# A mixture of experts in one order by load: dense, 128-slot and 64-slot members in place of nine equal ones

## What is computed

```python
def moe_swiglu(h, router, w_gate, w_up, w_down):
    logits = (hf @ router).astype(jnp.float32)
    top_v, top_i = lax.top_k(logits, TOP_K)          # 2 of 8
    top_w = jax.nn.softmax(top_v, axis=-1)
    # gates: for each token the two weights, at its two experts
    for e in range(N_EXPERTS):
        y = y + gates[:, e:e + 1] * swiglu(hf, w_gate[e], w_up[e], w_down[e])
```

## Time and profile before

| | us |
|---|---|
| median of 3 runs | 1819.85 (1819.36 to 1824.78) |
| profiled execution | 1821.17 |
| its span | 1819.4 |
| first expert product on PE | 901.57 |
| last down product on PE | 1797.11 |

### The profile page before, as it was taken

The page is one execution under the profiler, slowest core; times in us unless marked ns, Lnnn a source line. Parts: engine busy times, 40 slices in busy tenths (PEclk is TensorE's granted clock), DMA queues, the critical chain, the costliest instruction groups (busy, mean ns, idle before and its releaser), DMA issues.

```text
span 1819.4 us, 20970 instructions
## 1 busy us (share of the span) xinstructions
PE 1689.4 (93%) x8417; PEld 1387.7 (76%) x8418; DVE 1388.9 (76%) x1442; ACT 910.9 (50%) x837; POOL 0.2 (0%) x4
## 2 busy tenths in 40 slices
PE   4988999999999797797799999999999999999995
PEld 1876777788888596466688888888888888888884
DVE  5858657776777845674488988889798989888896
ACT  5431232211122334332477777777677777777773
POOL 0000000000000000000000000000000000000000
PEclk9988999999999898899699999999999999999998
DMA  9533334444567132100299999999999999999992
GB/s 352 195 136 126 113 127 149 139 163 161 170 223 242 53 117 70 47 1 24 68 337 342 358 346 343 358 337 360 344 341 350 354 335 357 341 348 356 334 366 88
DMA packets 214552, 426.32 MB, mean 234 GB/s; under 512 B 8186, under 2 KB 64028, under 8 KB 214452
## 3 DMA queue, kind: packets, MB, share of 16 engines
q1 hardware_dynamic: 210218, 420.37, 65.9%
q10 hardware_dynamic: 4234, 4.57, 0.8%
HBM read 423.86 MB, written 1.05 MB: 234 GB/s over the span
## 4 chain that ended last, share of the span: by engine, by line
PE 88%; DVE 6%; ACT 2%; issue 1%; DMA 1%; SPq 1%; DVEq 0%; ACTq 0%
PE bank L504 26%; PE bank L506 25%; PE bank L505 25%; PE bank L1740 2%; PE bank L1795 2%; PE bank L1729 2%; DVE lo L463 2%; PE bank L1834 1%; PE bank L1515 1%; DMA raw<-in_ada_w_dram 1%; PE bank L1746 1%; PE bank L1509 1%; ACT hi L457 1%; PE bank L1868 0%; PE bank L1869 0%
## 5 line engine op out<-in xcount | busy, mean ns | idle before, releaser
L463 DVE TENSOR_TENSOR lo<-raw,hi 128x2048 fp32r<-128x2048 f32 x361 | 820.8, 2282 | 199.4 <-ACT hi L457 198.0
L457 ACT ACTIVATE hi<-raw 128x2048 fp32r<-128x2048 f32 x361 | 689.7, 1912 | 474.9 <-PE bank L506 454.3
L504 PE MATMUL bank<-hi,xgh 128*128 128x512 f32 (+1 forms) x864 | 328.8, 381 | 5.0 <-DVE lo L463 5.0
L506 PE MATMUL bank<-hi,xgl 128*128 128x512 f32 (+1 forms) x864 | 325.3, 377 | 0.0
L505 PE MATMUL bank<-lo,xgh 128*128 128x512 f32 (+1 forms) x864 | 325.3, 377 | 0.0
L504 PEld LDWEIGHTS bank<-hi,xgh 128*128 128x128 f32 x864 | 163.0, 189 | 36.6 <-issue 5.2
L506 PEld LDWEIGHTS bank<-hi,xgl 128*128 128x128 f32 x864 | 163.1, 189 | 33.0
L505 PEld LDWEIGHTS bank<-lo,xgh 128*128 128x128 f32 x864 | 163.1, 189 | 31.3
L504 PE MATMUL bank<-hi,aTh 128*128 128x512 f32 x396 | 159.0, 402 | 0.0
L506 PE MATMUL bank<-hi,aTl 128*128 128x512 f32 x396 | 154.7, 391 | 0.0
L505 PE MATMUL bank<-lo,aTh 128*128 128x512 f32 x396 | 154.4, 390 | 0.0
(11 more groups left out here) (315 smaller groups left out, 2188.8 us busy)
## 6 DMA issues: line engine op xcount, KB each, us to landing
raw<-in_moe_w_gate_dram SPq DMA_DIRECT2D x99, 1024.0 KB, 5.9
raw<-in_moe_w_up_dram SPq DMA_DIRECT2D x99, 1024.0 KB, 6.0
raw<-in_moe_w_down_dram SPq DMA_DIRECT2D x99, 1024.0 KB, 6.3
raw<-in_ada_w_dram SPq DMA_DIRECT2D x48, 1024.0 KB, 5.8
raw<-in_ffn_w_gate_dram SPq DMA_DIRECT2D x11, 1024.0 KB, 5.3
raw<-in_ffn_w_up_dram SPq DMA_DIRECT2D x11, 1024.0 KB, 5.3
raw<-in_ffn_w_down_dram SPq DMA_DIRECT2D x11, 1024.0 KB, 5.0
raw<-in_ab_w_in_dram SPq DMA_DIRECT2D x6, 1024.0 KB, 8.7
```

Of the source, the lines that this page charges most:

```text
L457: nc.scalar.activation(hi[n0 % SPL][:, 0:size], raw[slot][:, 0:size], ACT.Copy).then_inc(hi_ready, 1)
L463: nc.vector.tensor_tensor(lo[n0 % SPL][:, 0:size], raw[slot][:, 0:size], hi[n0 % SPL][:, 0:size].bitcast(F32), ALU.subtract).then_inc(lo_r ...
L504: nc.tensor.matmul(dst, lh, rh, start=first, stop=False, skip_group_check=True)
L506: return nc.tensor.matmul(dst, ll, rh, start=False, stop=last, skip_group_check=True)
```

## The change

The experts are ranked by their number of tokens on the chip. The rank is found by DVE (`order_i`), and SP reads it before it issues the first expert load (`order_ready`). The heaviest expert isn't gathered: its eleven chunks of 256 features are worked densely for all 256 tokens, weights stationary, tokens moving (`H3h`, `H3l`, split from `h2T`), with `heavy_features` and `heavy_down`; the chunks are placed between those of the others as HEAVY_AT says, (member, chunk): heavy chunk, and each heavy chunk adds its four results into `yM`. Ranks 1 to 3 have 128 slots and run as before, now unrolled. Ranks 4 to 7 have 64 slots: the stationary operand holds the `lo` and the `hi` tokens side by side, and two products a block do for three (`few_features`); both halves of the array's rows are added while the result is turned (`few_turn`, eight f32 products of 64 columns), and silu and the product come after the turn (`few_gate`, `few_product`, `few_hi`, `few_lo`). ACT copies the two banks of each chunk first (`few_copy`). The ninth member and the zero products before the first are gone; a loop `over` (a full 128-slot pass) remains for each expert that exceeds its slots. ACT and DVE walk one list of slabs p, with the small operations attached to the slab p - 3 or later that PE has then used (`back`). DVE forms H3 before the routing, finds both tiles' top two side by side, and subtracts `h2l` only after the order and the first `Pm`. The constants come by six small loads, the router's first, and the router's products wait for all six.

The diff, cut to its core:

```diff
+FEW = SLOTS // 2
+CAPS = (SEQ, SLOTS, SLOTS, SLOTS, FEW, FEW, FEW, FEW)
+LIGHT = range(1, NE)
+OVER = 3
+CHUNKS = FF // 256
+HEAVY_AT = {(1, 0): 0, (4, 1): 1, (4, 3): 2, (4, 4): 3, (5, 1): 4, (5, 3): 5, (5, 4): 6, (6, 1): 7, (6, 3): 8, (7, 1): 9, (7, 3): 10}
...
+def moe_slabs():
+
+    order = []
+    for w in LIGHT:
+        for c in range(6):
+            n = HEAVY_AT.get((w, c))
+            parts = 2 if c < 5 else 1
+            order += [("hg", n), ("hu", n)] if n is not None else []
+            order += [(w, first_slab("g", c) + q) for q in range(parts)]
+            order += [("hd", n)] if n is not None else []
+            order += [(w, first_slab("u", c) + q) for q in range(parts)]
+        order += [(w, 22 + j) for j in range(11)]
+    return order
+
...
+            sp.wait_ge(order_ready, 1)
+            heaviest = sp.value_load(order_i[0:1, 0:1], min_val=0, max_val=NE - 1)
+            e, e_of = None, 0
+            for kind, n in MOE:
+                if kind == "hg":
+                    load(sp, "moe", (kind, n), mw["g"][bass.ds(heaviest, 1), :, :, 256 * n:256 * n + 256].rearrange("e p k f -> p (e k) f"))
+                elif kind == "hu":
+                    load(sp, "moe", (kind, n), mw["u"][bass.ds(heaviest, 1), :, :, 256 * n:256 * n + 256].rearrange("e p k f -> p (e k) f"))
+                elif kind == "hd":
+                    load(sp, "moe", (kind, n), mw["d"][bass.ds(heaviest, 1), :, 2 * n:2 * n + 2, :].rearrange("e p k f -> p (e k) f"))
+                else:
+                    if kind != e_of:
+                        e, e_of = sp.value_load(order_i[0:1, kind:kind + 1], min_val=0, max_val=NE - 1), kind
+                    light("moe", kind, n, e, 0)
...
+            def heavy_hi(n):
+
+                await_emptied(act, "moe", ("hu", n))
+                if n:
+                    full(act, "moe", ("hd", n - 1, 3))
+                nc.scalar.activation(hah[:], ham.rearrange("p (k s) -> p k s", k=2), ACT.Copy).then_inc(heavy_hi_done, 1)
...
+            for p in range(len(MOE) + SPL):
+                if p < len(MOE):
+                    split_hi(act, "moe", MOE[p])
+                w, s = back(p)
+                if w == "hg":
+                    heavy_silu(s)
+                if (w, s) == ("hu", 0):
+                    for h in range(2):
+                        gathered_hi("moe", 1, h)
+                    for h in range(2):
+                        gathered_lo("moe", 1, h)
+                    gathered_places("moe", 1)
+                if back(p, 1)[0] == "hu":
+                    heavy_hi(back(p, 1)[1])
...
+            chain.mark(V.memset(zeros[:], 0.0))
+            for h in range(2):
+                for k in range(4 * h, 4 * h + 4):
+                    await_emptied(dve, "norm3", k)
+                hi_lo(H3h[:, 4 * h:4 * h + 4, :], H3l[:, 4 * h:4 * h + 4, :], h2T[:, 4 * h:4 * h + 4, :], h3_ready)
...
+            def heavy_product(n):
+
+                await_emptied(dve, "moe", ("hg", n))
+                b = full(dve, "moe", ("hu", n))
+                if n:
+                    dve.wait_ge(heavy_lo_done, n)
+                emptied(V.tensor_tensor(ham, b[:], hsg, ALU.mult), "moe", ("hu", n))
+
+            def heavy_lo(n):
+
+                dve.wait_ge(heavy_hi_done, n + 1)
+                V.tensor_tensor(hal[:], ham.rearrange("p (k s) -> p k s", k=2), hah[:].bitcast(F32), ALU.subtract).then_inc(heavy_lo_done, 1)
+
+            def heavy_add(n, outs):
+
+                for o in outs:
+                    t, h = o // 2, o % 2
+                    b = full(dve, "moe", ("hd", n, o))
+                    y = yM[:, t, 512 * h:512 * h + 512]
+                    emptied(V.scalar_tensor_tensor(out=y, in0=b[:], scalar=gate_r[:, t, 0:1], in1=y, op0=ALU.mult, op1=ALU.add),
+                            "moe", ("hd", n, o))
...
+            for p in range(len(MOE) + SPL):
+                if p < len(MOE):
+                    split_lo(dve, "moe", MOE[p])
+                w, s = back(p)
+                if w == "hu":
+                    heavy_product(s)
+                if back(p, 1)[0] == "hu":
+                    heavy_lo(back(p, 1)[1])
+                if w == "hd":
+                    heavy_add(s, range(2))
+                if back(p, 1)[0] == "hd":
...
+            def few_features(kind, w, c):
+
+                n_ = 512 if c < 5 else 256
+                b = bank(pe, "moe", (kind, w, c))
+                parts = 2 if c < 5 else 1
+                for q in range(parts):
+                    blocks = KD // parts
+                    wh, wl = slab(pe, "moe", (w, first_slab(kind, c) + q), (blocks, n_))
+                    for k in range(blocks):
+                        kk = q * blocks + k
+                        T.matmul(b[:, 0:n_], xg[:, kk, 0:P], wh[:, k, :], start=(kk == 0), stop=False, skip_group_check=True)
+                        ins = T.matmul(b[:, 0:n_], xg[:, kk, FEW:FEW + P], wl[:, k, :], start=False, stop=(kk == KD - 1),
+                                       skip_group_check=True)
+                    used(ins)
...
+            def few_turn(w, c):
+
+                n_ = 4 if c < 5 else 2
+                await_emptied(pe, "moe", ("g", w, c))
+                await_emptied(pe, "moe", ("u", w, c))
+                b = bank(pe, "moe", ("t", w, c))
+                for i, src in enumerate((sge, ame)):
+                    for j in range(n_):
+                        c0 = (i * n_ + j) * FEW
+                        ins = T.matmul(b[:, c0:c0 + FEW], src[:, c % 2, j * P:(j + 1) * P], pair[:], start=True, stop=True)
+                filled(ins, "moe", ("t", w, c))
...
+            def heavy_features(kind, n):
+
+                b = bank(pe, "moe", (kind, n))
+                wh, wl = slab(pe, "moe", (kind, n), (KD, 256))
+                for b_ in range(2):
+                    for k in range(KD):
+                        cols = slice(b_ * P, (b_ + 1) * P)
+                        ins = product(pe, b[:, 256 * b_:256 * b_ + 256], wh[:, k, cols], wl[:, k, cols], H3h[:, k, :], H3l[:, k, :],
+                                      k == 0, k == KD - 1)
+                used(ins)
+
+            def heavy_down(n):
+
+                pe.wait_ge(heavy_lo_done, n + 1)
+                wh, wl = slab(pe, "moe", ("hd", n), (2, D))
+                for o in range(4):
+                    t, h = o // 2, o % 2
+                    b = bank(pe, "moe", ("hd", n, o))
+                    for k in range(2):
+                        toks, cols = slice(t * P, (t + 1) * P), slice(512 * h, 512 * h + 512)
+                        ins = product(pe, b[:], hah[:, k, toks], hal[:, k, toks], wh[:, k, cols], wl[:, k, cols], k == 0, k == 1)
+                    if o < 3:
+                        filled(ins, "moe", ("hd", n, o))
+                used(ins)
+
...
+            pe.wait_ge(h3_ready, 2)
+            for w in LIGHT:
+                few = CAPS[w] == FEW
                 for c in range(6):
-                    features(st, "g", w, c, it)
-                    features(st, "u", w, c, it)
-                    if c == 0 and st == "moe":
+                    n = HEAVY_AT.get((w, c))
+                    if n is not None:
+                        heavy_features("hg", n)
+                        heavy_features("hu", n)
+                    if (w, c) == (1, 0):
+                        for b_ in range(4):
+                            await_emptied(pe, "route", ("back", b_))
+                        pe.wait_ge(p_ready, 2)
+                        for part in ("xh", "xl"):
+                            for h in range(2):
+                                gather_rows("moe", part, 1, h, 1)
+                        gather_places("moe", 1, 1)
+                    if c == 0:
+                        arrived("moe", w)
+                        if w == 4:
+                            pe.wait_ge(zeroed, 2)
+                    for kind in "gu":
+                        if few:
+                            few_features(kind, w, c)
+                        else:
+                            features("moe", kind, w, c)
+                        if kind == "g" and n is not None:
+                            heavy_down(n)
+                    if c == 0 and w > 1:
                         for h in range(2):
-                            await_emptied(pe, st, ("d", 1 - w, h), it, lag=1 - w)
-                        scatter(st, w, 1 - w, it)
-                    if c == 0 and st == "ninth":
+                            await_emptied(pe, "moe", ("d", w - 1, h))
+                        scatter("moe", w - 1, (w - 1) % 2)
+                    if c and few:
+                        few_turn(w, c - 1)
+                    elif c:
+                        turn("moe", w, c - 1)
+                down_e("moe", w)
```

More of the change, by code:

```diff
@@ L172, in bank_order, with last_slab, heavy_in @@
[L172 to L176, removed]
+    def last_slab(kind, c):
+        return first_slab(kind, c) + (1 if c < 5 else 0)
+    def heavy_in(n, c):
```

(38 more changed lines are left out.)

617 lines of the change are left out of this document (378 added, 239 removed).

## The result

The changed kernel takes 1854.05 us (median of 4 runs, 1850.28 to 1860.31) against 1819.61 before: ratio 1.0187, 95% interval 1.0172 to 1.0202. It is slower by 1.9%, where I had forecast 1.5% faster. Its profiled execution has a span of 1848.4 us, where my sum gave 1792.9.

What follows compares the result with a forecast made beforehand. PE was taken to set the pace before the change. Member 4's start at 1220.8, 550 for members 4 to 7 and 22.1 to the end gave a span of 1792.9, adjusted to 1793.4 us; range 1740 to 1836.

Steps and rivals of the forecast that it cites:

- The start: First expert product on PE, after ranking and the first weight load: at 898.0 us, against 901.6 before.
- members 1 and 2: Expert stage: 124.1 us for the first member with its heavy chunk, 99.7 for the second.
- part 2: Heavy chunks, members 4 to 7: queue order makes PE stand 4.3 us before heavy_down; with waits 537.6 us.
- Rival (a): Members 4 to 7: the heavy chunks' waits are absorbed, 452 us instead of 550; 1695 in all, chance 12%.
- Part 3: PE clock after stands before heavy_down: half of ten fall to half clock, 2.4 us each; 12 us, bounds 0 and 24.
- rival (b): Clock falls at each stall, stays down through heavy_down and two slabs: about 60 us instead of 12; 1841, chance 13%.
- its sign: Granted clock under 0.9 over 1250 to 1750 us would show the clock staying down after stalls.
- Part 1: Totals without waiting for members 4 to 7: PE 450 us, DVE 430, DMA 452.
- Part 4: Start and experts 1 to 3: member 4 starts at 1220.8 us; overflow, place and zeroing cost at most 3.
- the long stretches: Between heavy chunks DVE paces at 2.20 us a slab; 43.1 us for seventeen slabs into the next expert.
- rival (c): DVE-paced stretches: ACT's hi comes late, 0.25 us a slab on 88 slabs, 22 us; 1815, chance 13%.
- (d): An expert overflows its slots and an extra pass of 99.7 us plus 4 runs: 1897, chance 2%.

Runs made afterwards that it cites:

- experiment 1: Changed kernel with heavy_product, heavy_hi and heavy_lo moved ahead of the split of the same step in ACT's and DVE's queues: 1800.44 us, ratio 0.9887.
- experiment 6: Changed kernel with heavy_product, heavy_hi, heavy_lo and heavy_add ahead of the splits, and the waits on the two zeroings apart: 1770.38 us, ratio 0.9721.
- experiment 2: Changed kernel with sixteen useless 512-column products put before each heavy_down but the first: 1828.56 us, ratio 1.0043.
- Experiment 3: Changed kernel without the gate half of few_turn's f32 products, so the output is not the reference's: 1831.80 us, ratio 1.0052.
- experiment 10: Changed kernel with useless products before each heavy_down but the first, half of few_turn's products left out and the zeroing's waits apart: 1803.53 us, ratio 0.9887.
- experiment 5: Changed kernel with only the placing changed, all eleven heavy chunks in members 1 to 3: 1812.44 us, ratio 0.9940.

## Why the prediction was wrong

**What held.** The start (895.5 for 898.0), members 1 and 2 to within 3 us, and above all part 2: PE stood 4.05 to 4.4 us before each `heavy_down` (4.3 to 4.6 forecast), released by `hal`, and waited for the additions before `few_turn` (15.4 us in ten). DVE idled 11.9 to 15.4 us in the 31 us from each hg on (12 forecast). That these waits, and not the totals, decide was the right step; experiments 1 and 6 show it. Rival (a), the totals, was out by 159 us.

**Part 3, the clock, mis-sized.** I counted a fall in half of the stands and 2.4 us each, 12 us. All ten fell, nine chunks had a second fall, and experiment 2 gives 26 us: 14 too few. This is also rival (b), in part: the clock came back during `heavy_down` rather than after it, and its sign (under 0.9 over 1250 to 1750) did not show, at 0.92.

**Part 1 and 2, `few_turn`, mis-sized.** 0.94 us for 1.70, since two instructions make one f32 product. Part 1 had it in PE's total, and part 2 had none of it on the path, as hidden where DVE paces. Experiment 3 takes out 0.85 a turn, and gains 24 us: at 1.70 it was not hidden.

**Part 4, "nothing on the path, at most 3 us".** I had put the zeroing in DVE's slack. The operation is short (0.88 us), but I looked only at DVE's load and not at who waits for it and what is queued ahead. It cost 5 to 9 us. `overflow`, at the end of member 2, took most of the 2.8 us by which this member was longer than 99.7, and together the two are well above my 3. In seven of the experiments' profiled executions the clock fell to half for 3.4 us behind the same stand of 1.95 us, and the member took 103.7 to 104.0. DVE takes 20 small operations in a row, from the one shown to 1118.5, and PE waits behind them for the next `lo`:

```profile
1114.86 0.16 DVE L1541 TENSOR_TENSOR over<-load_key,order_f 128x8 f32<-128x8 f32 x1
...
1120.94 0.47 PE L563 MATMUL bank<-hi,aT 128*128 128x512 f32 x1 [1.95 <-DVE lo L522]
```

**Part 2, the long stretches.** With all of this out (experiment 10), the first takes 77.0 instead of 72.5, and three members together some 12 us more. In that run DVE is all but gapless there, as forecast, with one wait for `hi` of 0.61 us in the first stretch. But PE starts the next member's hg 1.75 us after its `lo` is there:

```profile
1384.00 6.68 DVE L522 TENSOR_TENSOR lo<-raw,hi 128x2048 fp32r<-128x2048 f32 x3
```

```profile
1388.30 0.39 PE L2162 MATMUL bank<-yeh,PT 128*128 128x512 f32 x1
...
1390.15 0.28 PE L563 MATMUL bank<-H3h,hi 128*128 128x256 f32 x1
```

The second of DVE's three splits is that of hg and ends at about 1388.4; PE then has the scatter in hand, until 1390.15. Part 1 had the scatter in PE's total (1.9), part 2 left it out. It explains some 5 of the 12 us; the clock was at half once more in two of the chunks (3.4 us each), and waits for `hi` beyond the forecast sum to 3 or 4 us. So rival (c) had a small share of what it was priced at. This split is read from the trace alone, with no run of its own.

Sum: 14 for the clock, 21 for the turn (24 x 0.76 / 0.85, the part that I had left out), 7 for the zeroing, 3 for `overflow`, 12 for the stretches: 57 against 60.7 (1854.05 less 1793.4). The terms were got from differences of runs with intervals of some 3 us each and overlap in places (some turns ran at half clock), so the match is closer than it deserves to be.

Two small slips changed nothing: part 2 has PE go on at about T+14 without waits, where its own terms give T+11, and part 4 took the last down product at 1797.3, where the earlier trace rows have 1797.11.

**The range** was too narrow above for a reason that can be named: each of the terms that I had missed or counted too low was an extra wait or slower work, and none of them was a gain. I had placed the chance of slower at 0.16, on rivals (b) and (d) and a bit of (c), where five small terms of the same sign in a forecast of 27 us gain were enough.

## What to carry to other kernels

Where work is cut down on an engine, the time follows only if that engine doesn't then wait for its neighbours: here a third of the products of four members was worth nothing until the heavy chunks' small operations stood ahead of the splits in their queues, and 41 us after that. An operation that the pacing engine waits for belongs ahead of the bulk work of the same step, and the stands of 4 us on PE cost more than themselves here, as the products behind them ran at half clock. What PE does between two stretches, as the scatter, belongs on the path of the stretch paced by another engine. When a price is read from a row with a count, check how many instructions one operation of the program makes.

## What the runs showed of the hardware that I had not expected

An f32 product of 64 columns with a stationary operand of 128 x 128 stands as two instructions in the trace and takes 0.21 us at full clock, nearly as long as a product of 512 columns in the fast format (0.233). Each of ten stands of 4.05 to 4.4 us was followed by half clock for some products. Of eleven stands of 2.2 us ahead of `heavy_down` (experiment 5) seven were; stands of 1.3 to 1.6 us there (14.6 us in ten, experiment 6) were followed by none, at a mean granted clock of 1.00.
